# A hybrid decoder layer on one Trainium2 core: gate projection steps moved out of the attention into the RWKV inverse, carry and scan

## The reference, cut to what matters

```python
p = h @ w_in                                   # q | k | v | rwkv features | gate_a | gate_b
q, k, v, p_rw, g_a, g_b = jnp.split(p, IN_SPLITS, axis=-1)
o_a = swa_prompt(q, k, v, sinks, t5_table)     # 256 prompt rows; softmax with a sink column
o_a_s = swa_sample(q, k, v, cache_k, cache_v, sinks, t5_table)     # 8 sample rows
o_b, new_wkv = rwkv7_mix(p_rw, rw_prev, rw_wkv, *lw['rw'])         # lax.scan of the step below
m = sigmoid(g_a) * (o_a @ w_pa) + sigmoid(g_b) * (o_b @ w_pb)
x = x + gt1 * (m @ w_o)
x = x + gt2 * moe_ffn(h2, ...)                 # top 4 of 32 experts, 12 MB of weights each

def rwkv7_step(S, inp):
    r_t, w_t, k_t, v_t, kk_t, a_t = inp
    sa = jnp.einsum('bhvk,bhk->bhv', S, -kk_t)
    S = S * w_t[:, :, None, :] + sa[..., None] * (kk_t * a_t)[:, :, None, :] + v_t[..., None] * k_t[:, :, None, :]
    return S, jnp.einsum('bhvk,bhk->bhv', S, r_t)
```

## Time and profile before

| quantity | before |
|---|---|
| median of 3 runs | 1295.73 us (1293.49 to 1296.33) |
| profiled execution, its own time | 1295.52 us |
| span of the profile | 1293.7 us |
| PE busy | 1243.3 us, 96% |
| DVE, ACT, POOL busy | 446.1, 296.8, 53.3 us |
| HBM read | 463.91 MB |
| chain that ended last | PE 77%, DMA 18%, ACT 2%, DVE 2%, issue 1% |

### The profile page before, as it was taken

The page is one execution under the profiler, slowest core; times in us unless marked ns, Lnnn a source line. Parts: engine busy times, 40 slices in busy tenths (PEclk is TensorE's granted clock), DMA queues, the critical chain, the costliest instruction groups (busy, mean ns, idle before and its releaser), DMA issues.

```text
span 1293.7 us, 21059 instructions
## 1 busy us (share of the span) xinstructions
PE 1243.3 (96%) x8371; PEld 619.1 (48%) x8371; DVE 446.1 (34%) x1035; ACT 296.8 (23%) x548; POOL 53.3 (4%) x67
## 2 busy tenths in 40 slices
PE   7999998899999999999999999999999999999998
PEld 5787786788743333333333333333333333333343
DVE  2145747546353222233322223332222223332232
ACT  3012441220232221122222112222211122221211
POOL 0010622200000000000000000000000000000000
PEclk9999998999999999999999999999999999999999
DMA  9976352148689999999999999999999999999995
GB/s 362 364 255 249 115 158 76 36 149 308 252 354 404 427 428 428 429 430 428 427 429 429 428 429 429 428 428 428 429 428 429 429 428 427 429 429 427 429 427 226
DMA packets 55613, 467.14 MB, mean 361 GB/s; under 512 B 5142, under 2 KB 7450, under 8 KB 29691
## 3 DMA queue, kind: packets, MB, share of 16 engines
q1 hardware_dynamic: 53354, 461.07, 85.9%
q0 software_dynamic: 1664, 5.20, 1.5%
q10 hardware_dynamic: 544, 0.13, 0.0%
HBM read 463.91 MB, written 5.09 MB: 363 GB/s over the span
## 4 chain that ended last, share of the span: by engine, by line
PE 77%; DMA 18%; ACT 2%; DVE 2%; issue 1%; SPq 0%; DVEq 0%
PE ps L1415 26%; DMA ring<-in_w 15%; PE ps L1436 14%; PE ps L1359 6%; PE ps L900 5%; PE ps L1384 4%; PE ps L890 4%; DMA ring<-in_w_in 2%; PE ps L1304 2%; PE ps L1272 2%; PE ps L1424 2%; PE ps L1366 1%; ACT PT L766 1%; PE ps L909 1%; PE ps L869 1%
## 5 line engine op out<-in xcount | busy, mean ns | idle before, releaser
L1415 PE MATMUL ps<-ring,PT 128*64 128x512 f32 x1536 | 337.3, 593 | 7.1 <-DMA ring<-in_w 6.8
L1970 DVE TENSOR_TENSOR SQ<-ps,SQ 128x528 f32<-128x528 f32 x124 | 79.1, 700 | 590.9 <-PE ps L1384 590.9
L1415 PEld LDWEIGHTS ps<-ring,PT 128*64 128x64 f32 x1536 | 109.8, 137 | 227.9 <-issue 210.4
L1436 PE MATMUL ps<-ring,PT 128*64 128x512 f32 x768 | 170.1, 595 | 0.0
L761 ACT COPY HT<-ps 128x512 f32<-128x512 f32 x62 | 33.3, 589 | 369.4 <-PE ps L1415 369.4
L1415 PE MATMUL ps<-arena,PT 128*64 128x512 f32 x512 | 113.5, 593 | 1.7 <-DMA arena<-in_w 1.7
L1436 PEld LDWEIGHTS ps<-ring,PT 128*64 128x64 f32 x768 | 53.2, 137 | 99.8 <-issue 99.8
L1359 PE MATMUL ps<-XR,PT 128*64 128x512 f32 (+1 forms) x384 | 94.1, 607 | 0.1
L1415 PEld LDWEIGHTS ps<-arena,PT 128*64 128x64 f32 x512 | 37.6, 137 | 74.0 <-issue 68.7
L1384 PE MATMUL ps<-PT 64*128 64x264 f32 x496 | 71.7, 408 | 0.0
L900 PE MATMUL ps<-HT,ring 128*128 128x264 f32 x304 | 69.3, 388 | 0.0
(11 more groups left out here) (457 smaller groups left out, 1154.8 us busy)
## 6 DMA issues: line engine op xcount, KB each, us to landing
ring<-in_w SPq DMA_DIRECT2D x144, 2048.0 KB, 27.1
arena<-in_w SPq DMA_DIRECT2D x48, 2048.0 KB, 27.7
ring<-in_w_mod SPq DMA_DIRECT2D x12, 2048.0 KB, 15.0
ring<-in_w_in SPq DMA_DIRECT2D x9, 2048.0 KB, 14.6
ring<-in_w_o SPq DMA_DIRECT2D x2, 2048.0 KB, 11.1
ring<-in_w_pa SPq DMA_DIRECT2D x1, 2048.0 KB, 9.1
ring<-in_w_pb SPq DMA_DIRECT2D x1, 2048.0 KB, 8.4
bias_rows<-bias_by_distance POOLq DMA_DIRECT2D x1, 1536.0 KB, 13.8
```

The costliest lines, as they stand in the source:

```text
L1415: last = mm(ps[64 * lin:64 * lin + 64, 2 + hh, :], XG[:, k % 4, k // 4, :], slot_tile(slot, c)[:, k % 2, lin * FE + hh * 512:lin * FE + hh ...
L1436: last = mm(ps[64 * hh:64 * hh + 64, 4, :], AC[:, f, :], slot_tile(slot, c)[:, f % 4, hh * 512:hh * 512 + 512], start=(f == 0), stop=(f == ...
L1970: v.tensor_tensor(YA[:, p::4, :], ps[:, bank:bank + 2, 0:T], YA[:, p::4, :], ALU.add).then_inc(sem["comb_used"], 1)
```

## The change

The 104 gate steps stay, but stand elsewhere. The numbers in order are now 8 ahead of the attention; 8, 8, 8, 8, 3, 1, 10, 2 (48) in it; 4 after the token rows; 5, 4, 3 among the A/B products and the first Y; 1 after Y and 2 between the halves in levels 2 to 5 (12); 4 and 4 at XZW; 2, 2, 1, 2, 1 in the carry; 2, 1, 1 in the scan. Banks and the order of ACT's `gates(b)` follow. The keys x values products move into level 1. The two products that accumulate into one place in the carry, and the two of the outputs in the scan, are issued as two passes over all heads and chunks with `start` only at the first product of a bank. The scaling of the attention probabilities moves from DVE to ACT. Eight small products of the sample queries become two. The sample state's last two steps are split into four parts that run in levels 1 to 4; `sample_output` runs after the levels; the copy `OS` comes ahead of one state addition. `stream` has ("mod", 9) ahead of ("win", 7), with `mod9` and `win7` both in slot 0.

```diff
-        stream += [("win", win, 5), ("win", win, 6), ("win", win, 7), ("mod", wmod, 9), ("win", win, 8),
+        stream += [("win", win, 5), ("win", win, 6), ("mod", wmod, 9), ("win", win, 7), ("win", win, 8),
-        slots_of = [0, 1, 2, 3] + [4, 0, 1, 2, 3, 0, 1, 2, 0, 1] + [0, 1, 0, 1, 1, 0, 3, 2, 1, 4, 5]
+        slots_of = [0, 1, 2, 3] + [4, 0, 1, 2, 3, 0, 1, 2, 0, 1] + [0, 1, 0, 0, 1, 0, 3, 2, 1, 4, 5]
-        GATE_BANK = [4, 5, 7, 5, 7, 5, 7, 5, 7, 0, 3, 3, 2]
+        GATE_BANK = [4, 5, 7, 5, 7, 0, 7, 1, 3, 7, 3, 7, 0]
...
+                act.wait_ge(sem["att_sum"], g4 + 1)
+                for g in range(4):
+                    ins = act.mul(Pm[:, g, 0:J], Pm[:, g, 0:J], st[:, 8 + g:9 + g])
+                ins.then_inc(sem["att_p"], 1)
...
-            for h in range(HQ):
-                s = h % 2
-                last = mm(ps[:, 2 + s, NS * (h // 2):NS * (h // 2) + NS], II[64 * s:64 * s + 64, :], PTv[64 * s:64 * s + 64, h // 2, NP:T],
+            for s in range(2):
+                last = mm(ps[:, 2 + s, 0:4 * NS].rearrange("p (a b) -> p a b", b=NS), II[64 * s:64 * s + 64, :], PTv[64 * s:64 * s + 64, 0:4, NP:T],
...
             scores(0)
-            gates(12)
+            gates(8)
             pe.wait_ge(sem["qs_evac"], 1)
             scores(1)
-            gates(12)
+            gates(8)
             probabilities(0)
             scores(2)
             values(0)
-            gates(16)
+            gates(8)
             probabilities(1)
             scores(3)
             values(1)
-            gates(16)
+            gates(8)
+            pe.wait_ge(sem["att_max"], 3)
+            gates(3)
             probabilities(2)
             gates(1)
             values(2)
-            gates(12)
+            gates(10)
             probabilities(3)
-            gates(3)
+            gates(2)
             values(3)
...
             pe.wait_ge(sem["row_evac"], 8)
-            gates(10)
+            gates(4)
...
-                    gates(4)
+                    gates(5)
...
-                if n == 0:
-                    gates(2)
+                gates(4 - n)
+            pe.wait_ge(sem["f_evac"], 8)
+
+            def keys_values(n):
+
+                for h, par in quads:
+                    u, q = 8 * n + h, other(h, par)
+                    col = 4 * n * CH + in_group(h) * CH
+                    last = mm(ps[64 * q:64 * q + 64, 7 if q != par else 3, col:col + CH], half(KR, par)[:, u, 0:CH],
+                              half(Vr, par)[:, u, :], start=True, stop=True)
+                last.then_inc(sem["u0_done"], 1)
...
+                if i == 1:
+                    pe.wait_ge(sem["f_evac"], 9)
+                    keys_values(0)
+                elif i == 2:
+                    pe.wait_ge(sem["u0_evac"], 2)
+                    gates(1)
+                else:
+                    gates(1)
...
+                    if n == 0:
+                        if i == 1:
+                            keys_values(1)
+                        else:
+                            gates(2)
...
+            for h, c in allu:
+                mm(head_chunk(2, h, c), rows_of(Kr, h, c, 0, CH), rows_of(Vr, h, c, 0, CH), start=first_in_bank(h, c), stop=False)
+            pe.wait_ge(sem["dr_ready"], 2)
+            gates(1)
+            for h, c in allu:
+                last = mm(head_chunk(2, h, c), rows_of(Br, h, c, 0, CH), rows_of(XZW, h, c, CH, P), start=False, stop=last_in_bank(h, c))
             last.then_inc(sem["carry_done"], 1)
...
+            for h, c in allu:
+                mm(head_chunk(4, h, c), rows_of(Vr, h, c, 0, CH), rows_of(KR, h, c, CH, P), start=first_in_bank(h, c), stop=False)
+            gates(1)
+            for h, c in allu:
+                last = mm(head_chunk(4, h, c), rows_of(XZW, h, c, CH, P), rows_of(NR, h, c, CH, P), start=False, stop=last_in_bank(h, c))
+            last.then_inc(sem["o_done"], 1)
...
             chain(v.tensor_tensor(S0, S0, over_values(1), ALU.mult))
+            dve.wait_ge(sem["smp_done"], 3)
+            done(v.tensor_copy(OS[:, :, :], ps[:, 4, 0:64].rearrange("p (a b) -> p a b", b=HQ)), "smp_att", 4)
             dve.wait_ge(sem["smp_part"], 1)
             chain(v.tensor_tensor(S0, S0, T2, ALU.add))
-            dve.wait_ge(sem["smp_done"], 3)
-            done(v.tensor_copy(OS[:, :, :], ps[:, 4, 0:64].rearrange("p (a b) -> p a b", b=HQ)), "smp_att", 4)
-            chain(v.tensor_tensor(T1, over_keys(sa), over_values(2), ALU.mult))
...
                 if i < 5:
-                    sample_output(i - 1)
+                    sample_state(i - 1)
+            for part in range(4):
+                sample_output(part)
             bonus()
```

More of the change, by code:

```diff
@@ L1170, in _ @@
                     last.then_inc(sem["dx_done"], 1)
-            pe.wait_ge(sem["f_evac"], GATES - 1)
-            for n in range(2):
-                for h, par in quads:
-                    u, q = 8 * n + h, other(h, par)
-                    col = in_group(h) * CH
-                    last = mm(ps[64 * q:64 * q + 64, 4 * n + (1 if q != par else 3), col:col + CH], half(KR, par)[:, u, 0:CH],
-                              half(Vr, par)[:, u, :], start=True, stop=True)
-                last.then_inc(sem["u0_done"], 1)
+                    if n == 0:
+                        if i == 1:
+                            keys_values(1)
+                        else:
+                            gates(2)
             for n in range(2):
                 pe.wait_ge(sem["xx_ready"], 2 * (len(LEVELS) - 1) + n + 1)
-                pe.wait_ge(sem["u0_evac"], n + 1)
                 for h, par in quads:
@@ L1206, in _, with first_in_bank, last_in_bank @@
             last.then_inc(sem["carry_done"], 1)
-            pe.wait_ge(sem["f_evac"], GATES)
-            for h, c in allu:
-                mm(head_chunk(2, h, c), rows_of(Br, h, c, 0, CH), rows_of(XZW, h, c, CH, P), start=True, stop=False)
-                last = mm(head_chunk(2, h, c), rows_of(Kr, h, c, 0, CH), rows_of(Vr, h, c, 0, CH), start=False, stop=True)
+            gates(2)
+            def first_in_bank(h, c):
+                return h < 2 and c < 2
+            def last_in_bank(h, c):
+                return h >= HQ - 2 and c >= NCHUNK - 2
@@ L1222, in _ @@
+            gates(1)
+            for h, c in allu:
+                last = mm(head_chunk(4, h, c), rows_of(XZW, h, c, CH, P), rows_of(NR, h, c, CH, P), start=False, stop=last_in_bank(h, c))
+            last.then_inc(sem["o_done"], 1)
+            pe.wait_ge(sem["f_evac"], 12)
+            for c in range(1, NCHUNK):
+                pe.wait_ge(sem["g_ready"], c)
                 for h in range(HQ):
                     s, hp = h % 2, h // 2
-                    out = head_chunk(4, h, c)
-                    mm(out, rows_of(XZW, h, c, CH, P), rows_of(NR, h, c, CH, P), start=True, stop=False)
@@ L1226, in _ @@
-                    last = mm(out, rows_of(Vr, h, c, 0, CH), rows_of(KR, h, c, CH, P), start=False, stop=True)
-                for h in range(HQ if c else 0):
+                    last = mm(ps[64 * s:64 * s + 64, 7, hp * CH:hp * CH + CH], MC[64 * s:64 * s + 64, hp, c, :],
+                              G4[64 * s:64 * s + 64, c - 1, hp, :], start=True, stop=True)
+                last.then_inc(sem["gm_done"], 1)
+                for h in range(HQ):
                     s, hp = h % 2, h // 2
@@ L1682, in _ @@
                 dve.wait_ge(sem["att_exp"], 4 * g4 + 4)
-                chain(v.reciprocal(st[:, 8:12], st[:, 8:12]))
-                for g in range(4):
-                    ins = v.tensor_scalar(Pm[:, g, 0:J], Pm[:, g, 0:J], st[:, 8 + g:9 + g], None, ALU.mult)
-                    if g == 3:
-                        done(ins, "att_p", g4 + 1)
+                v.reciprocal(st[:, 8:12], st[:, 8:12]).then_inc(sem["att_sum"], 1)
                 if g4 < 3:
```

60 lines of the change are left out of this document (32 added, 28 removed).

## The result

The kernel after takes 1287.28 us (median of 6 runs, 1285.52 to 1290.35), the kernel before in the runs beside it 1294.61 (1291.26 to 1296.86): a ratio of 0.9943 with a 95% interval of 0.9929 to 0.9956. It is faster by 7.3 us, where 12.2 were forecast. The profiled execution took 1286.5 us against 1295.52.

What follows compares the result with a forecast made beforehand. Never-resting expert weight transfers, started by PE's arrival at the projection, were taken to bound the kernel. Stages -9.4 - 6.1 + 1.55 - 1.4 + 3.2 = -12.15 from 1295.5 gave 1283.3 us, own range 1280 to 1287.5, wider range 1279.5 to 1291.5.

Steps and rivals of the forecast that it cites:

- What bounds the kernel: Expert weight transfers never rest; PE's arrival at the projection (272.24) moves the end by the same amount.
- Attention: 140.17 to 184.08: 24 gate steps leave, fewer sample passes, waits come up by 2.1; -9.4 us (bounds -11.5 and -5).
- The slower rival, the softmax chain: Attention set by DVE addition, ACT exponentials and scaling, PE transposes in series; 1300.2 us, chance 0.06.
- Token rows: Sample attention and token rows, 184.08 to 210.54: shorter copy wait, six steps leave; -6.1 us (bounds -7.1 and -3.5).
- its one guess: Token rows: one slow-clock stretch of half the old length returns, charged 1.0 us.
- A/B products to first Y: 210.54 to 220.44: twelve steps instead of 6, +2.74, of which 1.2 fit in waits; +1.55 us (bounds 0 and +2.7).
- Levels: 220.44 to 252.01: 984 passes, 7.7 instruction blocks, laid out as 29.85 us; -1.4 us (bounds -6.5 and +5.5).
- the feed: PE's instruction supply in blocks of some 256, priced at 3.77 us at least, about 1.4 more with a transfer.
- Nearly free: Where passes are short and the feed binds, a gate step, 4 instructions for 0.457 us, costs almost nothing.
- The rival that the feed does not bind: Levels cost PE's 24.6 us of work and the transfers' 1.4 and 0.3 go; 1276.4 us, chance 0.09.
- XZW, carry, scan: 252.01 to 272.24: twelve more steps +5.5, two-pass products -1.5, `w_pa` block +1.4; +3.2 us (bounds 0 and +6.5).
- Paid in full: Rival: the RWKV part pays for its 24 steps in full, +11.0 against -9.4 in attention; 1290.8 us, chance 0.19.

Runs made afterwards that it cites:

- the run with waits in the attention: Kernel after, with four long-satisfied waits ahead of each of 44 gate steps in the attention: 1287.03 us, 0.9918 of the kernel before.
- the repeat: The unchanged kernel after, measured again on the chip shared with three follow-up kernels: 1287.05 us, 0.9931 of the kernel before.
- the runs with two and four waits: Kernel after, with two or four long-satisfied waits ahead of every second short product of levels 2 to 5: 1293.72 us (0.9986) and 1310.85 us (1.0121).
- the kernel with the copy first: Kernel before, with only the copy `OS` moved ahead of the S0 addition: 1292.26 us against 1296.73, 0.9973.
- the run with empty levels: Kernel after, with the twelve gate steps of the levels moved behind the XZW products, six to each half: 1290.11 us, 0.9959 of the kernel before.
- Y issued twice: Kernel after, with the products Y of levels 2 to 5 issued twice into the same place: 1294.39 us, 0.9990 of the kernel before.

## Why the prediction was right and where it was wrong

The direction, the place of the gain and the range held: 1287.28 lies between 1279.5 and 1291.5, near the upper end of the forecast's own range of 1280 to 1287.5. It is 4.0 us over the 1283.3; by the profiled executions 3.0 are missing (-9.16 instead of -12.15, the median beside them 0.8 more). All of it lies in two stages, A/B products and XZW to scan. That the levels came out to 0.03 us is luck, as is said there.

**What bounds the kernel: right.** The experts kept their period to 0.01 us, and the 8.2 us that PE gained ahead of the projection came off the end, one for one within the scatter of the part behind it (1016.8 to 1020.4 us).

**Attention, -9.4 forecast, -9.8 measured: right.** The transposes were put at 174.7 and stand at 175.21, with the stage beginning 0.94 later. ACT's scaling was taken at 1.3 us; it is 1.28 for half a row and 1.70 for a full one. PE's waits are 0.80, 0.28 and 0.51, 1.6 in all instead of 2.1. The slower rival, the softmax chain, asked for a scaling of over 3 us and fell. The gain that I held possible in the first group is real, 3.4 us on the engine: with the scaling on DVE, PE waits 2.28 us there. No run put the 24 steps back; that their leaving is what shortened the stage rests on their price and the rows. The same attention took 33.90 to 35.52 us in the profiles without a half-clock stretch in it, by the race between DVE and POOL, which the prediction didn't have among its terms.

**Token rows, -6.1 forecast, -6.0 measured: right, with its one guess.** Without a half-clock stretch I had -7.1, and the run with waits in the attention shows -7.2; I charged 1.0 for a returning stretch of half the old length. It returned at full length, 6.8 us, cost 1.15 here (20.43 - 19.28), for DVE's copies hid the rest, and went on into the next stage, where nothing was charged. That it returned was my guess and not derived: in two other kernels it stayed away.

**A/B products to first Y, +1.55 forecast, +2.9 measured: the size failed.** The clock is the larger part: 3.01 instead of 1.98 us for the first products. In the repeat and in the runs with two and four waits, where the clock is full from the start of this stage or nearly, it is 11.76 to 11.79, +1.9, 0.35 over the forecast. That rest is the waits of the kernel before: they hold 0.85 us (0.53 and 0.32 for DVE), where I let 1.2 of the steps vanish in them.

**Levels, -1.4 forecast, -1.4 measured: right in sum by luck, half right in reason.** Unchanged levels take 29.21 to 31.08 us from one execution to the next, and those of the kernel before, which are 31.57 in its profile, 30.07 in the kernel with the copy first; so -1.4 can't be told from +1.0 or -2.4. I let the feed set all of it, with 24.6 us of work beneath, 19.1 of short products and 5.5 of steps. The work is 27.97. Both terms were too low. The short products alone are 21.77 us in the run with empty levels, among them 32 passes DX at 1.03 (223.93 to 224.96), where 0.85 was taken. And the price of a step: 0.457 us is its share in a row of 16; between short products one alone takes 0.65 and a pair 1.08, so twelve are 6.9 us, or 6.2 by the same run, not 5.5. Part of the excess was hidden, since the feed leaves idle time: of 6.2 us more work 2.5 disappeared. "Nearly free" was wrong; "3.75 a block" was right, as Y issued twice shows. That the clock would be full here, where it was 0.89, I had not counted at all, and it is part of why the sum came out. The rival that the feed does not bind (1276.4) asked for levels of 24.6 us, and they take 30.2; but it fell by the work as much as by the feed. The page "Runtime: NRT & Kernel Launch" of the Trainium skill, section Instruction fetch mechanics, calls the crossing mostly hidden; with long passes the runs agree, with passes of 16 to 18 ns they show it in the open.

**XZW, carry, scan, +3.2 forecast, +5.2 measured: the size failed.** The mechanism of the transfer was right: w_pa lengthens one block, 1.59 us where 1.4 was charged, and taking it away takes the stall away; only the issue came at 249.25, 5 us sooner than the 254 that I gave. Without it the stage is still +3.3 where the forecast without it would be +1.8. By the rows: twelve steps in four pairs and four singles are 4 x 1.09 + 4 x 0.64 = 6.9, not 5.5; the scan hides less than I took, the turn with two steps being 2.12 instead of 1.7, though of the 2.4 us of steps in it 1.95 are hidden; the two passes bring 1.0 to 1.2 (17.8 ns for a pass against 22.5 before, not 15.9), not 1.5. The 0.41 at XZW that I took off here was a mistake of the stages: that wait lies ahead of 252.01, so it is part of the levels. What did go here, and stood nowhere in the sum, is the issue stall of 0.93 at 262.74 of the kernel before. 6.9 - 1.95 - 1.1 - 0.93 = 2.9, against 3.3 measured; 0.4 stays open. DVE was in time for the carry additions, as forecast.

**Paid in full (1290.8)** came nearer to the median than 1283.3 by 0.5 us only in number: its mechanism, no hiding in the levels, would have given +5.5 there. The measured time lies between the two because each was half right: 2.5 of 6.2 us of steps are hidden in the levels, 1.95 of 6.9 in the carry and scan.

## What to carry to other kernels

Price a filler step where it will stand, not from a long run of its kind: here it cost 0.46 us in a row of sixteen, 0.54 in a pair and 0.65 alone among short products. Where passes are short, count instructions as well as microseconds, take the larger, and keep bulk transfers out of that stretch, since a weight load issued one stage later was worth 2.3 us without any other change. Before moving work between stages, look for an engine's small operation queued behind a large one: exchanging two statements alone gave 3.5 us by the ratio, where this whole change gives 7 to 9. And profile the same kernel more than once before a difference of a microsecond in one stage is given a cause.

## What the runs showed of the hardware

- A satisfied wait costs PE nothing that the runs tell apart when it is the only one ahead of a product. When one stays as an instruction of its own it costs 0.04 us on the mean and up to 0.09, and when two do 0.13 and up to 0.20, between products of 0.03 us. In front of gate steps it nearly disappears (0.12 us for 88).
- Where short products leave PE short of instructions, its longer stalls lie exactly 256 passes and weight loads apart, or a multiple of that, and 3.3 to 3.9 us pass for 256 (5.33 in one block of the kernel before). In one run 3.75 us for each gave 36.3 of 36.8 us; beside a transfer of 2 MB it stopped for 1.6 us even where PE asks for less (586 passes in 25 us are 4.6 blocks, 5.4 us each).
- In the token rows the clock fell to 0.50 half a microsecond into a wait of 2.54 us, in the kernel after 0.06 us before a wait of 0.21 began, and in two other kernels with that wait not at all. What PE does ahead of it is much the same in all of these; what decides was not found, and no run here was aimed at it.
- Four DVE scalings of 128x128 take 4.69 us beside two of POOL's products and 1.09 where they meet only the end of one; on ACT they take 1.28 beside the same work. A DVE step of 128x4 takes 0.34 us when it starts ahead of such a product and 2.33 when it starts 0.06 us behind it, which lengthened the attention by some 1.4 us in two of the profiles.
